# Rounded products in the mixers' last stage: three-part scores, and values weighed by pairs of heads

## The reference

```
def dsa_mixer(q, c_kv, iq, ik, iw, kv_norm, w_uk, w_uv):
    c = rmsnorm(c_kv, kv_norm)
    q_lat = jnp.einsum('bthd,hdc->bthc', qh, w_uk) * HEAD_DIM ** -0.5
    ...
        logits = jnp.einsum('bqhc,bqkc->bqhk', q_lat_b, c_sel).astype(jnp.float32)
        logits = jnp.where(valid[:, :, None, :], logits, -jnp.inf)
        prob = jax.nn.softmax(logits, axis=-1).astype(c.dtype)
        o_lat = jnp.einsum('bqhk,bqkc->bqhc', prob, c_sel)
        return jnp.einsum('bqhc,hcd->bqhd', o_lat, w_uv)
```

## Time and profile before

| | |
|---|---|
| median of 3 runs | 3670.35 us (3665.62 to 3674.88) |
| the profiled execution: own time, span | 3665.43 us, 3663.6 us |
| TensorE busy, VectorE busy, over the whole span | 97%, 55% |
| the stage in the first layer | 2055.4 to 2143.4 us of the span |
| in it: up to the first evicted unit | 25.0 us, VectorE busy 9.05 |
| the loop to the last evicted unit | 53.3 us, VectorE busy 35.66 |
| the same loop in the second layer (3190.0 to 3243.2) | 53.2 us, VectorE busy 35.62 |
| from the last evicted unit to the end of the stage | 9.7 us, VectorE busy 4.49 |

### The profile page before, as it was taken

How to read it: one execution, slowest core, us unless ns; L and a number is a source line. 1 busy time by engine, 2 the same in 40 slices (tenths; PEclk the granted TensorE clock), 3 DMA queues, 4 the chain that set the end, 5 groups by cost and what they waited for, 6 DMA issues and landing times. The chain is left out here.

```text
span 3663.6 us, 61588 instructions
## 1 busy us (share of the span) xinstructions
PE 3566.1 (97%) x26295; PEld 3092.2 (84%) x26295; DVE 2024.6 (55%) x3372; ACT 1430.8 (39%) x2289; POOL 176.9 (5%) x220
## 2 busy tenths in 40 slices
PE   9999999899999999999999999999999999999998
PEld 8999999788899998888877678888888877678887
DVE  7667663544476646544478564444444468664443
ACT  6844332554453323322244353223232244353222
POOL 0000000111000001000004100000000004100000
PEclk9999999999999999999999999999999999999999
DMA  3232333122223332333320023333333320023332
GB/s 137 81 99 81 93 88 92 65 77 76 68 71 93 91 90 80 98 97 95 115 75 3 24 81 98 98 91 105 95 96 94 111 86 3 24 70 98 98 93 80
DMA packets 87873, 303.22 MB, mean 83 GB/s; under 512 B 9632, under 2 KB 11808, under 8 KB 87344
## 3 DMA queue, kind: packets, MB, share of 16 engines
q1 hardware_dynamic: 87600, 299.28, 26.6%
HBM read 297.11 MB, written 2.13 MB: 82 GB/s over the span
## 5 line engine op out<-in xcount | busy, mean ns | idle before, releaser
L698 DVE TENSOR_TENSOR two_w_lo<-one_raw,two_w_hi 128x1024 fp32r<-128x1024 f32 (+1 forms) x333 | 399.3, 1200 | 749.9 <-ACT two_w_hi L690 747.7
L713 PE MATMUL psum<-two_x_hi,two_w_hi 128*128 128x512 f32 x1768 | 695.1, 393 | 1.1 <-DVE two_rows L1592 0.9
L713 PE MATMUL psum<-two_x_hi,two_w_lo 128*128 128x512 f32 x1768 | 688.4, 389 | 0.0
L713 PE MATMUL psum<-two_x_lo,two_w_hi 128*128 128x512 f32 x1768 | 688.0, 389 | 0.0
L690 ACT CAST two_w_hi<-one_raw 128x1024 fp32r<-128x1024 f32 (+1 forms) x333 | 340.9, 1025 | 803.0 <-PE psum L713 803.0
L713 PEld LDWEIGHTS psum<-two_x_hi,two_w_hi 128*128 128x128 f32 x1768 | 331.8, 188 | 91.3 <-issue 22.1
L2404 PE MATMUL psum<-one_x_hi,one_w_hi 128*128 128x264 f32 (+1 forms) x1376 | 391.6, 285 | 7.9 <-DVE one_x_lo L798 7.3
L713 PEld LDWEIGHTS psum<-two_x_hi,two_w_lo 128*128 128x128 f32 x1768 | 331.9, 188 | 69.7
L713 PEld LDWEIGHTS psum<-two_x_lo,two_w_hi 128*128 128x128 f32 x1768 | 332.0, 188 | 69.5 <-issue 1.4
L2404 PE MATMUL psum<-one_x_lo,one_w_hi 128*128 128x264 f32 (+1 forms) x1376 | 389.3, 283 | 0.0
L2404 PE MATMUL psum<-one_x_hi,one_w_lo 128*128 128x264 f32 (+1 forms) x1376 | 388.7, 282 | 0.0
(11 more groups left out here) (563 smaller groups left out, 6733.9 us busy)
## 6 DMA issues: line engine op xcount, KB each, us to landing
one_raw<-in_swi_in SPq DMA_DIRECT2D x172, 512.0 KB, 3.6
one_raw<-in_ffn_in SPq DMA_DIRECT2D x88, 512.0 KB, 3.8
one_raw<-in_swi_out SPq DMA_DIRECT2D x64, 448.0 KB, 3.3
one_raw<-in_mix_in SPq DMA_DIRECT2D x54, 512.0 KB, 3.6
one_raw<-in_attn_w SPq DMA_DIRECT2D x32, 512.0 KB, 3.9
one_raw<-in_swi_out SPq DMA_DIRECT2D x32, 512.0 KB, 3.6
one_raw<-in_ffn_out SPq DMA_DIRECT2D x32, 448.0 KB, 3.3
one_raw<-in_lru_w SPq DMA_DIRECT2D x24, 512.0 KB, 5.2
```

What stands on the lines that cost most here:

```text
L698: self.nc.vector.tensor_tensor(lo, self.m.raw[:, u % self.RAW, 0:self.cols(u)], hi.bitcast(FP32), ALU.subtract).then_inc(self.s["w_lo"], 1)
L713: last = self.nc.tensor.matmul(self.m.ps[:, bank, :], a[:, w], b[:, k0 + k, :], start=(start and k == 0 and q == 0), stop=(stop and k == n ...
```

## The change

The scores of a unit become three products with rounded operands. `q_lo`, `c_lo` are what rounding leaves over of the queries and the latents; ScalarE writes the rounded ones where it wrote the queries (`q_hi`) or in a new copy (`c_hi`), and VectorE subtracts (`query_rest`, six times; one instruction for `c_lo`). A bank of latent queries is now free only when VectorE has read it too.

The turned probabilities and `c_tok` are split in the same manner: ScalarE copies the rounded part out as before, and VectorE subtracts it from the bank (`turned_rest`, once for each unit, one unit behind; one instruction for `c_tok`). Two heads of a block share a buffer, and `attend` now takes a pair of heads at once: three products of 256 columns for each block of keys, in place of one for each head. `keep` copies a pair. `attend_at` puts a pair's products two units behind its second head. At the end of the loop, `finish` moves: the first pair of heads behind the last transposes, the other two behind the last attend.

The diff, with buffers' addresses and lines that repeat left out:

```
         self.olat = m.high[:, 0:6 * SEQ].rearrange("p (n t) -> p n t", t=SEQ)
-        self.probT = [slot(m.high, 10 + j) for j in range(2)]
-        self.c_tok = slot(m.high, 12).rearrange("p (n f) -> p n f", f=P)
+        self.probT = m.late_p
+        self.c_tok = m.late_tok
...
+    groups = [(b, h) for b in range(NB) for h in range(0, H, 2)]
+    NG = len(groups)
+    attend_at = {g: min(H * b + h + 3, NA - 1 if g < NG - 1 else NA) for g, (b, h) in enumerate(groups)}
...
                     pe.wait_ge(s["q_out"], h - 1)
+                    pe.wait_ge(s["q_rest"], h - 1)
...
-                        pe.wait_ge(s["c_ready"], 1)
-                        pe.wait_ge(s["q_out"], h + 1)
-                    nc.tensor.matmul(m.ps[:, bank(i), 0:(b + 1) * QB], e.qlat[:, h, b * QB:(b + 1) * QB],
-                                     c_lat[:, 0:(b + 1) * QB], start=True, stop=True).then_inc(s["scored"], 1)
+                        pe.wait_ge(s["c_rest"], 1)
+                        pe.wait_ge(s["q_rest"], h + 1)
+                    out, queries, n = m.ps[:, bank(i), 0:(b + 1) * QB], slice(b * QB, (b + 1) * QB), (b + 1) * QB
+                    nc.tensor.matmul(out, e.q_lo[h][:, queries], e.c_hi[:, 0:n], start=True, stop=False)
+                    nc.tensor.matmul(out, e.q_hi[h][:, queries], e.c_hi[:, 0:n], start=False, stop=False)
+                    nc.tensor.matmul(out, e.q_hi[h][:, queries], e.c_lo[:, 0:n], start=False, stop=True).then_inc(
+                        s["scored"], 1)
...
-                    pe.wait_ge(s["probT_ready"], u - 1)
+                    pe.wait_ge(s["probT_rest"], u - 1)
...
+            def attend(g):
+                b, h = groups[g]
+                pe.wait_ge(s["probT_rest"], H * b + h + 2)
+                if g >= 2:
+                    pe.wait_ge(s["out_ready"], g - 1)
+                out = m.ps[:, 4 + g % 2, 0:2 * QB].rearrange("p (h t) -> p h t", t=QB)
+                probs = e.probT[g % 2]
                 for n in range(b + 1):
-                    last = nc.tensor.matmul(m.ps[:, 4 + u % 2, 0:QB], e.c_tok[:, n, :],
-                                            e.probT[u % 2][:, n * QB:(n + 1) * QB], start=(n == 0), stop=(n == b))
+                    keys_of = slice(n * QB, (n + 1) * QB)
+                    nc.tensor.matmul(out, e.c_tok.lo[:, n, :], probs.hi[:, :, keys_of], start=(n == 0), stop=False)
+                    nc.tensor.matmul(out, e.c_tok.hi[:, n, :], probs.hi[:, :, keys_of], start=False, stop=False)
+                    last = nc.tensor.matmul(out, e.c_tok.hi[:, n, :], probs.lo[:, :, keys_of], start=False, stop=(n == b))
                 last.then_inc(s["out_psum"], 1)
...
-            pe.wait_ge(s["q_out"], H)
+            pe.wait_ge(s["q_rest"], H)
             for c in range(C):
                 spread(m.ps[:, 2 + c, :], e.factor[:, 2 * NT * c:2 * NT * (c + 1)]).then_inc(s["spread"], 1)
...
-                elif u == NA - 2:
+                elif u == NA - 1:
                     pe.wait_ge(s["y_normed"], 2)
-                    pe.wait_ge(s["out_ready"], NA - 4)
+                    pe.wait_ge(s["out_ready"], NG - 2)
                     finish(0, 7)
-                elif u == NA - 1:
-                    pe.wait_ge(s["evicted"], N)
-                    pe.wait_ge(s["out_ready"], NA - 2)
-                    finish(1, 0)
-            attend(NA - 1)
-            pe.wait_ge(s["out_ready"], NA)
+            attend(NG - 1)
+            pe.wait_ge(s["evicted"], N)
+            pe.wait_ge(s["out_ready"], NG - 1)
+            finish(1, 0)
+            pe.wait_ge(s["out_ready"], NG)
             finish(2, 1)
...
             for h in range(2, H):
                 latent_query(h)
+            act.wait_ge(s["c_ready"], 1)
+            nc.scalar.copy(e.c_hi, c_lat).then_inc(s["c_rounded"], 1)
             act.wait_ge(s["c_psum"], 1)
...
+            def turned_rest(u):
                 b, h = dsa[u]
+                probs, n = e.probT[u // 2 % 2], (b + 1) * QB
+                dve.wait_ge(s["probT_ready"], u + 1)
+                nc.vector.tensor_tensor(probs.lo[:, u % 2, 0:n], m.ps[:, 2 + u % 2, 0:n], probs.hi[:, u % 2, 0:n].bitcast(FP32),
+                                        ALU.subtract).then_inc(s["probT_rest"], 1)
+
+            def keep(g):
+                b, h = groups[g]
+                dve.wait_ge(s["out_psum"], g + 1)
+                nc.vector.tensor_copy(e.olat[:, h:h + 2, b * QB:(b + 1) * QB], m.ps[:, 4 + g % 2, 0:2 * QB].rearrange(
+                    "p (h t) -> p h t", t=QB)).then_inc(s["out_ready"], 1)
+
+            def query_rest(h):
+                dve.wait_ge(s["q_out"], h + 1)
+                nc.vector.scalar_tensor_tensor(e.q_lo[h], m.ps[:, 2 + h % 2, :], SCALE, e.q_hi[h].bitcast(FP32), ALU.mult,
+                                               ALU.subtract).then_inc(s["q_rest"], 1)
...
-                if u >= 2:
-                    keep(u - 2)
+                if u:
+                    turned_rest(u - 1)
+                for g in range(NG):
+                    if attend_at[g] + 1 == u:
+                        keep(g)
...
-                elif u == NA - 1:
-                    dve.wait_ge(s["final_psum"], 1)
-                    nc.vector.tensor_copy(m.y[:, 3, 0:SEQ], m.ps[:, 7, :]).then_inc(s["done"], 1)
-            keep(NA - 2)
-            keep(NA - 1)
+            turned_rest(NA - 1)
+            keep(NG - 2)
+            keep(NG - 1)
+            dve.wait_ge(s["final_psum"], 1)
+            nc.vector.tensor_copy(m.y[:, 3, 0:SEQ], m.ps[:, 7, :]).then_inc(s["done"], 1)
             dve.wait_ge(s["final_psum"], 3)
```

More of the change, by code:

```diff
@@ L894, in part_two_memory @@
     m.ring = place("ring", [P, 2, 4 * KT * P], base + KT * T1 * 4 + (14 * SEQ + 384) * 4)
+    late = base + KT * T1 * 4
+    m.late_p = [Split(place("late_p_hi0", [P, 2, SEQ], late + 10 * SEQ * 4, FP32R),
+                      place("late_p_lo0", [P, 2, SEQ], hidden + 6 * SEQ * 4, FP32R)),
+                Split(place("late_p_hi1", [P, 2, SEQ], late + (17 * SEQ + 384) * 4, FP32R),
+                      place("late_p_lo1", [P, 2, SEQ], hidden + 8 * SEQ * 4, FP32R))]
+    m.late_tok = Split(*[place(f"late_tok_{n}", [P, SEQ // P, P], late + (12 + i) * SEQ * 4, FP32R) for i, n in enumerate(("hi", "lo"))])
+    m.late_q_hi = place("late_q_hi", [P, 6, SEQ], hidden, FP32R)
+    m.late_q_lo = [place("late_q_lo", [P, 5, SEQ], hidden + 60 * KB + 8 * 532 * 4, FP32R),
+                   place("late_q_lo5", [P, 1, SEQ], hidden + 60 * KB + 6 * 532 * 4, FP32R)]
+    m.late_c = Split(place("late_c_hi", [P, SEQ], base + KT * T1 * 4 + (19 * SEQ + 384) * 4, FP32R),
+                     place("late_c_lo", [P, SEQ], hidden + 52 * KB + 2 * SEQ * 4, FP32R))
 class Part:
@@ L3297, in __init__ @@
         slot = lambda t, i: t[:, i * SEQ:(i + 1) * SEQ]
-        self.qlat = m.low[:, 0:6 * SEQ].rearrange("p (n t) -> p n t", t=SEQ)
+        self.q_hi = [m.late_q_hi[:, h, :] for h in range(6)]
+        self.q_lo = [*[m.late_q_lo[0][:, h, :] for h in range(5)], m.late_q_lo[1][:, 0, :]]
+        self.c_hi, self.c_lo = m.late_c.hi[:, :], m.late_c.lo[:, :]
         self.olat = m.high[:, 0:6 * SEQ].rearrange("p (n t) -> p n t", t=SEQ)
         self.logits = [slot(m.high, 6 + j) for j in range(4)]
-        self.probT = [slot(m.high, 10 + j) for j in range(2)]
-        self.c_tok = slot(m.high, 12).rearrange("p (n f) -> p n f", f=P)
+        self.probT = m.late_p
+        self.c_tok = m.late_tok
         self.c_square = slot(m.high, 13)
@@ L3551, in _ @@
                 latent_query(h)
+            act.wait_ge(s["c_ready"], 1)
+            nc.scalar.copy(e.c_hi, c_lat).then_inc(s["c_rounded"], 1)
             act.wait_ge(s["c_psum"], 1)
[L3553 removed]
+            nc.scalar.copy(e.c_tok.hi[:, :, :], m.ps[:, 5, :].rearrange("p (n f) -> p n f", f=P)).then_inc(s["tok_ready"], 1)
             exponentiate(0)
@@ L3639, in _ @@
             nc.vector.reciprocal(e.factor, e.factor).then_inc(s["f_factor"], 1)
+            query_rest(2)
+            query_rest(3)
             evict(3)
+            query_rest(4)
+            query_rest(5)
+            dve.wait_ge(s["c_rounded"], 1)
+            nc.vector.tensor_tensor(e.c_lo, c_lat, e.c_hi.bitcast(FP32), ALU.subtract).then_inc(s["c_rest"], 1)
             dve.wait_ge(s["ahead_hi"], 1)
```

34 lines of the change are left out of this document (16 added, 18 removed).

## The result

The changed kernel takes 3683.56 us (median of 7 runs, 3680.08 to 3693.47) against 3670.35; the ratio is 1.0049, with a 95% interval of 1.0037 to 1.006. It is slower: by 13 us between the two medians, by 18 us by the ratio, which is taken over all runs. The profiled execution took 3680.08 us with a span of 3678.3 us, 14.65 us more than before; it is the fastest of the seven.

What follows compares the result with a forecast made beforehand. TensorE was taken to set the pace in the 512-key block, with VectorE becoming the bound there after the change. The terms summed to 3.4 us a layer, 6.8 for two, giving 3677.2 us from the 3670.35 median; range 3664 to 3690.

Steps and rivals of the forecast that it cites:

- the clock: Rival, chance 0.07: TensorE's pauses in each unit bring two more half-clock stretches a layer, 6.8 us on top, 3684 us.
- Same: Whole kernel measured between 3659.3 and 3681.4 us, not distinguishable from no change; chance 0.61.
- Ahead of the loop (+0.8): Before the loop, the query's remainder, `c_lo` and the weights' split start `normed` and the loop 0.8 us later a layer.
- First block (+0.4): Loop's first block: VectorE's added remainders, 0.20 in unit 1 and 0.33 in unit 4, cost 0.4 us a layer.
- 256 keys (+0.6): 256-key block: VectorE's additions of 1.5 us partly vanish in waits for scores, leaving 0.6 us a layer.
- 384 and 512 keys (+0.8 and +0.3): Last two blocks: VectorE's additions of 2.25 and 2.36 us nearly fit the stretches; gaps cost 0.8 and 0.3 a layer.
- the 1.62 us of a unit of before: 512-key block: VectorE's work per unit before the change, against TensorE's 2.19; with the additions it becomes 2.10 us.
- The remainder's price: On VectorE, a 512-column subtraction followed at once costs 0.60 us, not its full 0.689.
- TensorE's price: Rounded products start 0.23 us apart at 512 columns and 0.12 at 256; 0.12 was also taken for 128.
- The tail (+0.5, and the end 0): Last eviction to last scaling grows 0.5 us a layer; from there to the stage's last copy stays 7.2 us.
- the first rival (all of VectorE's additions): Rival, chance 0.23: in the loop nothing VectorE adds is absorbed, 16.4 us for two layers, 3686.8 us.
- the second (TensorE's gain): Rival, chance 0.15: remainders fall into idle time, the last two blocks shrink with TensorE, -2.7 us a layer, 3664.9 us.

Runs made afterwards that it cites:

- padded kernels: The changed kernel and the one before, each with eight of retention's sixteen pieces on the whole array by zero-filled copies: 3669.38 us and 3663.45 us.
- whole-array runs: The changed kernel and the one before, each with all retention products on the whole array, retention's result being another one: 3662.56 us and 3661.47 us.
- single 32-bit products: The changed kernel with each three rounded products replaced by one 32-bit product, the remainders made but not used: 3685.48 us, ratio 1.0047.
- GpSimd late: The changed kernel with GpSimd's nine operations on the first mixer's result held back until nine units have their probabilities: 3682.19 us, ratio 1.0048.

## Why the prediction was right, and where it was not

The time lies in the range, between the forecast (3677) and the upper end, and its sum was on the right side. Its reason is half of the story: the clock, which it had as a rival at 0.07, made half of the difference or more. That the range held nonetheless is in part luck. "Same" had 0.61 and "slower" by over 0.3% 0.36, and it became slower.

**Ahead of the loop (+0.8): not separable from the clock.** Where ScalarE and VectorE stand in the way the profile agrees: the split of the next weights ends at 2077.67 and `normed` starts at once, as in the working.

```profile
2076.45 1.22 DVE L3690 TENSOR_TENSOR two_ahead_lo<-two_ahead_raw,two_ahead_hi 128x1024 fp32r<-128x1024 f32 x1
2077.65 0.69 DVE L3694 TENSOR_TENSOR two_ring<-two_ring,psum 128x512 f32<-128x512 f32 x1
```

But against the earlier trace rows that is 2.5 us earlier, counted from VectorE's first operation of the stage, in the first layer (18.35 for 20.86) and 0.5 later in the second, by where spells fell. In the second layer this stretch had nearly the same clock (0.92 before, 0.93 now); there the first eviction comes 1.1 later (23.34 us for 22.24), which goes with the 0.8.

**First block (+0.4): mis-sized by the clock.** At full clock, the padded kernels differ by 0.1 and 0.4, so VectorE's part was priced rightly. Measured were +1.4 and +5.6.

**256 keys (+0.6): right, for another reason than I gave.** 11.84 against 11.40. The whole-array runs show that the cover was TensorE's half products: with these gone the additions cost 1.6, which is all of the 1.5 that I had counted.

**384 and 512 keys (+0.8 and +0.3): too high.** Measured +0.1 and -0.3. VectorE is the bound at 512 keys, as forecast:

```profile
2130.49 0.68 DVE L3624 CUSTOM_DVE_ANT_0 two_high<-psum,two_keys 128x512 f32<-128x512 f32 x1
...
2131.70 0.68 DVE L3645 TENSOR_TENSOR two_late_p_lo<-psum,two_late_p_hi 128x512 fp32r<-128x512 f32 x1
2132.30 0.68 DVE L3624 CUSTOM_DVE_ANT_0 two_high<-psum,two_keys 128x512 f32<-128x512 f32 x1
...
2133.50 0.68 DVE L3645 TENSOR_TENSOR two_late_p_lo<-psum,two_late_p_hi 128x512 fp32r<-128x512 f32 x1
...
2134.43 0.68 DVE L3624 CUSTOM_DVE_ANT_0 two_high<-psum,two_keys 128x512 f32<-128x512 f32 x1
...
2136.24 0.68 DVE L3624 CUSTOM_DVE_ANT_0 two_high<-psum,two_keys 128x512 f32<-128x512 f32 x1
```

The last three units take 1.81, 2.13 and 1.81, so 1.97 for a unit on average of the two kinds, not 2.1 to 2.2, and none waits for a score. The step that failed is the 1.62 us of a unit of before: I took it as solid work. From an eviction to the copy behind the scaling it took 1.33 then; from an eviction to the remainder it takes 1.20 now (2132.30 to 2133.50), and a unit with a remainder but no copy fits in 1.81. The remainder's price was right: 0.60 from its start to the next eviction (2131.70 to 2132.30), and its full 0.68 was not charged. The Trainium skill ("VectorE: DVE Perf Modes", section "The DRAIN you can't avoid") also says, beside the rule that the prediction took from it, that a next operation which is not held starts earlier; the trace goes with that. TensorE's price was right too, where products of one kind follow each other: scores start 0.23 apart and weighing 0.11 to 0.12, and 128 columns, for which no row stood, are 0.11 apart (3198.19 and 3198.30):

```profile
2132.69 0.28 PE L3438 MATMUL psum<-two_late_p_hi,two_late_tok_lo 128*128 128x256 f32 x1
2132.80 0.28 PE L3439 MATMUL psum<-two_late_p_hi,two_late_tok_hi 128*128 128x256 f32 x1
...
2133.41 0.40 PE L3408 MATMUL psum<-two_late_c_hi,two_late_q_lo 128*128 128x512 f32 x1
2133.64 0.39 PE L3409 MATMUL psum<-two_late_c_hi,two_late_q_hi 128*128 128x512 f32 x1
...
3198.19 0.28 PE L3409 MATMUL psum<-two_late_c_hi,two_late_q_hi 128*128 128x128 f32 x1
3198.30 0.28 PE L3410 MATMUL psum<-two_late_c_lo,two_late_q_hi 128*128 128x128 f32 x1
```

**The tail (+0.5, and the end 0): right in sum.** From the last eviction to the stage's end 10.19 us against 9.68: 0.3 of the growth lies ahead of the last scaling's end, and the end behind it is 7.38 against 7.2.

VectorE's waits now, as in the earlier trace rows, and below them TensorE's longest; the 5.8 us for scores are 3.3, and TensorE waits for probabilities (5.5, for 2.4 before), as forecast. VectorE's busy time in the loop grew by 6.3 us (41.95 for 35.65), where I had looked for some 8:

```profile
DVE two_high L3624 <- PE psum L3410: 3.3, 5, 1.4
DVE stat L3710 <- ACT two_high L3550: 1.6, 4, 0.6
...
PE psum L3425 <- DVE two_high L3714: 5.5, 8, 1.2
```

**The rivals.** The clock, to which I gave 0.07, is what happened, and its 3684 agrees only by luck: I expected two short spells in each layer from TensorE's pauses in the later blocks. These have 1.00 but for two windows (0.88 and 0.81 above, the second the end of the first block's spell); the spells grew in the first block, where I had seen the one of before and took its length (4 us) as fixed. That length is the step that had the clock wrong: it was up to 24 us. The Trainium skill ("TensorE: Matmul & The Clock Gate", section "A second HAM failure mode: psum-queue depth-cycling") blames pauses between groups of products. The spell shown above does begin behind one (0.93 us), but the whole-array run, with a pause of 1.66 us at 1.00, shows that a pause is not enough here. The sign that I had set for the first rival (all of VectorE's additions), units of the first block longer by more than 0.2, came true (0.23 and 0.93) and pointed the wrong way: at full clock, with padding, they are longer by 0.01 and 0.07. That rival holds only for 256 keys with padding; the second (TensorE's gain) falls by VectorE's pace at 512 keys, and by the single 32-bit products, which give TensorE's gain back at 3 us in all.

**The sum.** Of the 14.65 us between the profiled executions, the first two blocks make 10.3 (1.85 and 8.47). The other parts of the stage cancel (+0.3 a layer behind them, -1.9 and +1.1 ahead), and 4.5 us lie outside the stage, in code that is the same, where spells also shift between executions. With the first block at full or nearly full clock on both sides, the change costs 1.1 us (whole array) to 5.9 us (padded); the forecast's 6.8 stands just above that.

A second way to part the two: each run has its mean clock on record. The seven of the changed kernel have 0.982 to 0.987, those of the kernel before in the rounds of the experiments 0.987 to 0.991. Where both have 0.987, the changed kernel took 3680.08 and 3681.61 us and the one before 3672.25 to 3674.95 (five runs): some 7 us apart, as an estimate, since the clock is given to 0.001 only. By this, and by the padded pair, the change costs about what the forecast added up, and the lower clock comes on top.

**What stays open.** Why the kernel before gets out of a spell in 3 to 4 us and the changed one, with the same half products, in up to 24. Either half of the change is enough, and so are VectorE's additions with TensorE's old products; no single part could be named. What sets a spell off is open as well: with the whole array the same pauses had one in one layer and none in the other. Whether the half rows of retention's scores or the half columns of its weighing did the more was not tried apart. A product of span and mean clock, the 3629 of the expectations, proved good to 5 us only: 3676.8 x 0.986 = 3625 for GpSimd late, 3656.1 x 0.994 = 3634 for the whole array, with the same work.

## What to carry to other kernels

Where an edit moves a few tenths of a microsecond per unit, read the granted clock of each stretch before and after, and compare stretches at the same clock, before putting a difference down to an engine. Products on half of the array, mixed in with others, were dear twice here: the next product started later, and spells lasted longer with them. Zeros that fill the other half are worth trying where an idle engine can write them.

## What the runs showed of the hardware

- TensorE at half clock with no gap in its records for 24 us (3201 to 3225), and at full clock through 14 us with 3 us of gaps, in kernels that differ only in how much of the array some products use.
- Halves filled with zeros served much as data did: with padding six of eight first blocks stood at 1.00, with data in the whole array three of four, and with half products one of sixteen (GpSimd late, second layer).
- A half product of 256 columns delays what follows by 0.14 to 0.19 us against a whole one (0.63 and 0.57 for 0.44 and 0.43).
- A scaling of 128 columns on VectorE took 0.97 us beside one of GpSimd's TENSOR_TENSORs (1.26 us from 3199.50, so that both end within 0.1 us of each other), against 0.28 to 0.29 with GpSimd idle.
